# Mixed attention, linear attention and 32 experts on one core: the expert loop written out

## The chip, the cores and the metric

The kernel runs on one core of one Trainium2 chip. The metric is the device time of one execution, in microseconds (us), lower is better. The three timed executions of the kernel before took 1819.9, 1821.0 and 1821.1 us.

## What is computed

One layer over 512 tokens of width 1024, in float32: a mixer (chunked gated linear attention and three groups of dilated attention, gated and merged), then a mixture of experts, each behind a norm and with a residual. The change touches the experts alone:

```python
logits = (xn @ router_w + router_b).astype(jnp.float32)
top_v, top_e = lax.top_k(logits, TOP_K)          # 4 of 32 experts for each token
gates = jax.nn.softmax(top_v, axis=-1)
...
h = xb @ w_gate_up[e] + b_gate_up[e]             # 1024 -> 2048
gate = jnp.minimum(h[:, ::2], SWIGLU_LIMIT)
up = jnp.clip(h[:, 1::2], -SWIGLU_LIMIT, SWIGLU_LIMIT)
act = (up + 1.0) * (gate * jax.nn.sigmoid(SWIGLU_ALPHA * gate))
return act @ w_down[e] + b_down[e]               # 1024 -> 1024
```

Each token's four results are added with their gates as factors. Every expert has 8 MB of gate and up weights and 4 MB of down weights; the kernel reads all 32 experts' weights once, 384 MB.

## The kernel before, in words

The first 690 us or so are the mixer, the router and the lists of each expert's tokens. The expert stage is in `experts` (from L1820). An expert's tokens fill up to 96 slots; more are dealt with in `further_blocks`, behind a test, and that part is not touched.

Weights stream in 1 MB chunks through a ring of 16 buffers (`expert_ring`). An expert has twelve chunks, eight of gate and up and four of down. `chunk_loaded[r]` counts landings in slot r, and the semaphore `used` counts chunks that TensorE has read.

The stage runs in bodies, one for each of experts 0 to 30; expert 31 has an ending of its own. A body e is skewed: it multiplies gate and up of expert e + 1 (its chunks 0 to 7, `gate_up_chunk`, product line L1915) and then down of expert e (its chunks 8 to 11, `down_chunk`, L1924). Between them TensorE turns expert e's activations (`turn_act`, L1888) behind chunks 2 and 3, and expert e + 2's rows (`turn_rows`, L1878) behind chunk 9, where it also starts the next bias products (L1908). Each engine has a body of its own:

- TensorE (`body_pe`): the products above. Before a chunk it waits for its landing (`chunk_here`, L1745 and L1746), before the first for the copied rows (`x_out`), before the ninth for the activations (`aT_out`) and for the copied results of the body before (`y_out`).
- ScalarE (`body_act`): copies turned activations, the sigmoid, copies turned rows, and at the end scales the results out of PSUM (`rows_out`, L1981).
- VectorE (`body_dve`): the indices of expert e + 2 (`list_take`, `pieces_take`), then clamp and product of expert e + 1 (`swiglu`, L2001 and on).
- GpSimd: the gather of expert e + 2's rows (L1796), then the three scatters that add expert e's results in DRAM (L1870).
- SyncE: waits for `used`, then issues the chunk that goes 16 chunks further on (L1743); behind a body's ninth chunk, three small bias loads (L1737).

The order on each engine is written out by hand, and nothing but semaphores ties the engines together. The loop is made in `over_bodies`, for each engine on its own: bodies 0 and 1 are written out (`PEELED`), then a loop of 7 turns holds four bodies (`UNROLL`), then body 30 is written out. L2065 is the loop's `Fori`; its register set-up, addition and branch all stand under that line. In the loop every wait has a value worked out from the turn's number in a register; in bodies written out it is a constant.

```python
def over_bodies(engine, body):
    for e0 in range(PEELED):
        body(engine, e0, 0)
    with engine.Fori(0, TURNS) as i:
        for u in range(self.UNROLL):
            body(engine, PEELED + u, i)
    for e0 in range(PEELED + self.UNROLL * TURNS, LAST):
        body(engine, e0, 0)
```

Of the kernel before, what the change touches and what calls it, by code (L numbers as in the profile page):

```python
# [9 lines left out]
F32R = mybir.dt.float32r  # L10
I32 = mybir.dt.int32
# [5 lines left out]
P = 128  # L17
# [29 lines left out]
N_EXPERTS, TOP_K, FF = 32, 4, D_MODEL  # L47
# [79 lines left out]
class Kernel:  # L127
# [23 lines left out]
    def build(self):  # L151
        nc = self.nc
        with ExitStack() as top:
# [33 lines left out]
            with ExitStack() as late:  # L187
# [7 lines left out]
                with ExitStack() as moe:  # L195
# [11 lines left out]
                    first = [self.sb(moe, f"expert_chunk{j}", [P, 2, self.WIDE]) for j in range(self.GU)]  # L207
# [13 lines left out]
                    self.bias_place = self.sb(moe, "bias_place_r", [P, P], F32R)  # L221
                    self.index = [self.sb(moe, f"row_index{u}", [P, 1], I32) for u in range(self.UNROLL)]
                    self.piece_row = [self.sb(moe, f"piece_row{u}", [P, self.GROUPS], I32) for u in range(self.UNROLL)]
                    self.piece_weight = [self.sb(moe, f"piece_weight{u}", [P, self.GROUPS]) for u in range(self.UNROLL)]
                    self.moe = {n: self.sem("moe_" + n) for n in (
# [1489 lines left out]
    RING = 16  # L1715
    GU, PER_BODY, UNROLL = 8, 12, 4
    PER_TURN = PER_BODY * UNROLL
    PARTS, GROUPS = P // QUARTER, FIRST_SLOTS // QUARTER
# [25 lines left out]

    def chunk_here(self, pe, c, i=0):  # L1745
        pe.wait_ge(self.chunk_loaded[c % self.RING], 16 * (self.PER_TURN // self.RING) * i + 16 * (c // self.RING + 1))  # L1746
        return self.expert_ring[c % self.RING]
# [73 lines left out]
    def experts(self, stack):  # L1821
        nc, t = self.nc, self.t
        E, GU, BODY, TURN, RING = N_EXPERTS, self.GU, self.PER_BODY, self.PER_TURN, self.RING
        G, PARTS, PIECE, Q = self.GROUPS, self.PARTS, self.PIECE, QUARTER
        HELD = G * PIECE
        rows, y, a = (self.h[:, b, :] for b in range(3))
        xT, aT = self.rowsT, self.actT
        as_rows = lambda tile: tile[:].rearrange("p q k n -> p (q k) n")
# [14 lines left out]
        S = self.moe  # L1843
# [4 lines left out]
        part_rows = lambda p: slice(p * Q, (p + 1) * Q)  # L1848
# [55 lines left out]

        def gate_up_bias(pe, e0, i=0):
            pe.wait_ge(self.bias_in[e0 % 2], 16 * G * (self.UNROLL // 2) * i + 16 * G * (e0 // 2 + 1))
            for j, bank in enumerate(h_banks):
                pe.matmul(bank, self.bias_place[part_rows(j), :], self.bias_rows[e0 % 2][part_rows(j), :].bitcast(F32R),  # L1908
                          start=True, stop=False)

        def gate_up_chunk(pe, c, i, k, x=xT):
            w = chunk_here(pe, c, i)
            for j, bank in enumerate(h_banks):
                for p in range(PARTS):
                    last = pe.matmul(bank[part_rows(p), :], x[:, k, part_rows(j)], w[:, p // 2, p % 2 * COLS:(p % 2 + 1) * COLS],  # L1915
                                     start=False, stop=(k == KT - 1))
            last.then_inc(S["used"], 1)

        def down_chunk(pe, c, i, q):
            w = chunk_here(pe, c, i)  # L1920
            for kk in range(2):
                for j in range(G):
                    for p in range(PARTS):
                        last = pe.matmul(y_of(j)[part_rows(p), :], aT[:, q, kk, part_rows(j)], w[:, kk, p * PIECE:(p + 1) * PIECE],  # L1924
                                         start=(q == 0 and kk == 0), stop=(q == 3 and kk == 1))
            last.then_inc(S["used"], 1)
# [8 lines left out]

        def body_pe(pe, e0, i):
            e, more = i * self.UNROLL + e0, e0 < E - 2
            for q in range(BODY):
                c = self.body_chunk(e0, q)
                if q == 0:  # L1940
                    pe.wait_ge(S["x_out"], 2 * e + 4)
                    if e0 == 0:
                        pe.wait_ge(S["gu"], 2)
                        gate_up_bias(pe, 1)
                if q < GU:
                    gate_up_chunk(pe, c, i, q)
                else:
                    if q == GU:
                        pe.wait_ge(S["aT_out"], G * e + G)
                        if e0:  # L1950
                            pe.wait_ge(S["y_out"], G * e)
                    if q == BODY - 2 and e0 == E - 2:
                        turn_act(pe, E - 1, range(2))
                    if q == BODY - 1 and e0 == E - 2:
                        turn_act(pe, E - 1, range(2, G))
                    down_chunk(pe, c, i, q - GU)
                if q == 2:
                    turn_act(pe, e, range(2))
                if q == 3:
                    turn_act(pe, e, range(2, G))  # L1960
                if q == 9 and more:
                    turn_rows(pe, e + 2)
                    pe.wait_ge(S["gu"], 2 * e + 4)
                    gate_up_bias(pe, e0 + 2, i)

# [7 lines left out]

        def rows_out(act, e0, i):
            e = i * self.UNROLL + e0
            act.wait_ge(S["used"], TURN * i + self.body_chunk(e0, BODY - 1) + 1)
            act.wait_ge(S["pieces"], 2 * e + 2)
            if e0:
                act.wait_ge(S["scattered"], 16 * G * e)
            for j in range(G):  # L1980
                act.activation(y[:, j * PIECE:(j + 1) * PIECE], y_of(j), ACT.Copy,  # L1981
                               scale=self.piece_weight[e0 % self.UNROLL][:, j:j + 1]).then_inc(S["y_out"], 1)

        def body_act(act, e0, i):
            e = i * self.UNROLL + e0
            act_back(act, e, aT)
            gate_sigmoid(act, e + 1)
            if e0 < E - 2:
                rows_back(act, e + 2, xT)
            else:  # L1990
                act_back(act, E - 1, as_act(xT))
            rows_out(act, e0, i)

        def swiglu(dve, e, c, i, first=False):
            dve.wait_ge(S["used"], TURN * i + c + 1)
            if not first:
# [13 lines left out]

        def body_dve(dve, e0, i):
            e, more = i * self.UNROLL + e0, e0 < E - 2
            if more:
                u = (e0 + 2) % self.UNROLL
                if e0 > 1:
                    dve.wait_ge(S["scattered"], 16 * G * (e - 1))
                list_take(dve, e + 2, u)
                pieces_take(dve, e + 2, u)  # L2020
            else:
                list_hot(dve, E - 1)
            swiglu(dve, e + 1, self.body_chunk(e0, GU - 1), i)

# [33 lines left out]

        PEELED, LAST = 2, E - 1
        TURNS = (LAST - PEELED) // self.UNROLL  # L2060

        def over_bodies(engine, body):
            for e0 in range(PEELED):
                body(engine, e0, 0)
            with engine.Fori(0, TURNS) as i:  # L2065
                for u in range(self.UNROLL):
                    body(engine, PEELED + u, i)
            for e0 in range(PEELED + self.UNROLL * TURNS, LAST):
                body(engine, e0, 0)

        with nc.Block() as block:
            @block.sync
            def _(sp):
# [8 lines left out]

                def body(sp, e0, i):
                    e = i * self.UNROLL + e0
                    for q in range(BODY):
                        c = self.body_chunk(e0, q)
                        if c < RING:
                            continue
                        sp.wait_ge(S["used"], TURN * i + c - RING + 1)
                        if q < GU:  # L2090
                            self.load_gate_up(sp, c, e + 1, q)
                        else:
                            self.load_down(sp, c, e, q - GU)
                        if q == GU and e0 < E - 2:
                            self.load_bias_rows(sp, e + 2, e0)
                over_bodies(sp, body)
# [19 lines left out]
            def _(pool):  # L2116
# [20 lines left out]

                def body(pool, e0, i):
                    e = i * self.UNROLL + e0
                    if e0 < E - 2:  # L2140
                        gather(pool, e + 2, (e0 + 2) % self.UNROLL)
                    scatter(pool, e, e0 % self.UNROLL)
                over_bodies(pool, body)
# [29 lines left out]
            def _(dve):  # L2173
# [4 lines left out]
                dve.wait_ge(self.normed_stored, 16 * NB)  # L2178
                swiglu(dve, 0, GU - 1, 0, first=True)
                dve.wait_ge(S["lists_in"], 16 * (1 + PARTS))  # L2180
# [36 lines left out]
            def _(pe):  # L2217
# [9 lines left out]
                for c in range(GU):  # L2227
                    gate_up_chunk(pe, c, 0, c, as_rows(aT))
                    if c == 5:
# [288 lines left out]
```

## Time and profile before

| what | value |
|---|---|
| median of three executions | 1821.0 us |
| the profiled execution | 1832.8 us |
| its span, first to last instruction | 1831.0 us |
| mean granted TensorE clock | 0.985 |
| instructions executed | 38017 |
| weight traffic, hardware queue | 479.12 MB |

Rows of the profile are of one execution, which has its own time; a sum made from them is made against 1832.8 us. PE is a matmul of TensorE and PEld a weight load; PEldq, SPq, ACTq, DVEq and POOLq are the sequencers of the engines: waits, register work, branches and the issue of DMAs, which count as no busy time. "Issue" as the end of an idle time means that the engine waited for nothing that the profile shows. In the digits over 40 slices a slice is 45.8 us long. A float32 matmul of the program appears as two in the counts.

### The profile page before, as it was taken

How to read it: one execution, taken by the hardware profiler on the slowest of the kernel's cores; microseconds unless marked ns; L12 is line 12 of the kernel's file. 1: busy time of each engine (PE TensorE's matmuls, PEld its weight loads, DVE VectorE, ACT ScalarE, POOL GpSimd, SP SyncE). 2: the span in 40 equal slices, each digit the busy share in tenths (PEclk: the TensorE clock that was granted, in tenths of full speed). 3: DMA queues.
4: the chain of work that ended last, by engine and by line, in shares of the span. 5: the costliest groups of instructions: out<-in, count | busy, mean ns of one | idle time of the engine just before them, and what ended most of it. 6: DMA issues, size and time to landing. Idle time of an engine off the chain costs nothing.

```text
span 1831.0 us, 38017 instructions
## 1 busy us (share of the span) xinstructions
PE 1767.4 (97%) x16447; PEld 996.1 (54%) x16448; DVE 449.8 (25%) x692; ACT 378.9 (21%) x673; POOL 218.1 (12%) x182
## 2 busy tenths in 40 slices
PE   9999999999999989999999989989999989989997
PEld 7877788898888863433433433434334334334433
DVE  4256255446324540100100100100010001001003
ACT  4254232246422321110101111111111101101111
POOL 1000000000000013121112112112111211211111
PEclk9999999999999989999999999999999999999999
DMA  5321344412223787999989999999999999999973
GB/s 186 123 92 47 120 139 116 122 40 100 92 92 138 270 329 288 384 388 398 394 321 395 394 338 386 397 334 375 397 347 389 389 343 381 392 344 382 397 276 100
DMA packets 112158, 500.47 MB, mean 273 GB/s; under 512 B 19512, under 2 KB 29712, under 8 KB 62400
## 3 DMA queue, kind: packets, MB, share of 16 engines
q1 hardware_dynamic: 92272, 479.12, 68.4%
q0 software_dynamic: 18672, 16.74, 4.5%
q10 hardware_dynamic: 1056, 2.16, 0.5%
q8 instruction: 140, 2.29, 0.5%
q14 instruction: 18, 0.15, 0.0%
HBM read 486.07 MB, written 21.15 MB: 277 GB/s over the span
## 4 chain that ended last, share of the span: by engine, by line
PE 61%; issue 2%; DVE 0%; POOL 0%; ACT 0%; DVEq 0%
PE psum L1915 38%; PE psum L1924 18%; PE psum L1888 2%; PE psum L1878 1%; PE psum L1908 1%; PE psum L1932 1%; PE psum L244 0%; DVE expert_chunk L2056 0%; DVE h_sb L2212 0%; POOL total_rstd L2147 0%; PE psum L2045 0%; PE psum L2039 0%; ACT up_values L2168 0%; DVE gate_values L2212 0%; PE psum L2237 0%
## 5 line engine op out<-in xcount | busy, mean ns | idle before, releaser
L1915 PE MATMUL psum<-expert_chunk,rowsT 128*32 128x512 f32 x2976 | 341.9, 611 | 30.7 <-issue 30.7
L1915 PE MATMUL psum<-expert_chunk_late,rowsT 128*32 128x512 f32 x2976 | 328.5, 593 | 0.0
L2001 DVE TENSOR_SCALAR gate_values<-psum 128x768 f32<-128x768 f32 x32 | 30.6, 958 | 974.9 <-PE psum L1915 974.9
L1870 POOL DMA_INDIRECT residual_rows<-h_sb,piece_row x93 | 145.4, 1564 | 903.9 <-ACT h_sb L1981 830.0
L1915 PEld LDWEIGHTS psum<-expert_chunk,rowsT 128*32 128x32 f32 x2976 | 97.1, 112 | 243.9 <-issue 242.2
L1915 PEld LDWEIGHTS psum<-expert_chunk_late,rowsT 128*32 128x32 f32 x2976 | 93.4, 110 | 202.9 <-issue 200.5
L290 DVE TENSOR_TENSOR chunk_lo<-chunk,chunk_hi 128x2048 fp32r<-128x2048 f32 x48 | 110.0, 2291 | 257.5 <-ACT chunk_hi L286 238.7
L1924 PE MATMUL psum<-expert_chunk_late,activationsT 128*32 128x256 f32 x3072 | 172.2, 380 | 0.0
L1924 PE MATMUL psum<-expert_chunk,activationsT 128*32 128x256 f32 x2880 | 161.3, 380 | 0.0
L321 PE MATMUL psum<-xT_hi,chunk_hi 128*128 128x512 f32 x384 | 150.3, 392 | 4.5 <-DVE chunk_lo L290 2.0
L321 PE MATMUL psum<-xT_hi,chunk_lo 128*128 128x512 f32 x384 | 149.5, 389 | 0.0
L321 PE MATMUL psum<-xT_lo,chunk_hi 128*128 128x512 f32 x384 | 149.5, 389 | 0.0
L1924 PEld LDWEIGHTS psum<-expert_chunk_late,activationsT 128*32 128x32 f32 x3072 | 98.1, 110 | 73.8 <-issue 13.6
L286 ACT CAST chunk_hi<-chunk 128x2048 fp32r<-128x2048 f32 x48 | 91.8, 1913 | 189.5 <-PE psum L321 158.0
L1924 PEld LDWEIGHTS psum<-expert_chunk,activationsT 128*32 128x32 f32 x2880 | 92.1, 110 | 69.3 <-issue 12.6
L321 PE MATMUL psum<-chunk_hi,xT_hi 128*128 128x512 f32 x288 | 113.5, 394 | 2.6 <-ACT gla_v L723 1.5
L321 PE MATMUL psum<-chunk_hi,xT_lo 128*128 128x512 f32 x288 | 112.7, 391 | 0.0
L321 PE MATMUL psum<-chunk_lo,xT_hi 128*128 128x512 f32 x288 | 112.6, 391 | 0.0
L1900 ACT COPY activationsT<-psum 128x256 f32<-128x256 f32 x93 | 31.6, 374 | 338.6 <-PE psum L1888 305.0
L1972 ACT ACTIVATE gate_sigmoid<-gate_values 128x768 f32<-128x768 f32 x32 | 27.1, 847 | 350.0 <-DVE gate_values L2001 350.0
L321 PEld LDWEIGHTS psum<-xT_hi,chunk_hi 128*128 128x128 f32 x384 | 72.1, 188 | 21.3 <-DVE chunk_lo L290 2.7
L321 PEld LDWEIGHTS psum<-xT_hi,chunk_lo 128*128 128x128 f32 x384 | 72.1, 188 | 15.2
(281 smaller groups left out, 1533.1 us busy)
## 6 DMA issues: line engine op xcount, KB each, us to landing
expert_chunk<-in_expert_w_gate_up SPq DMA_DIRECT2D x132, 1024.0 KB
expert_chunk_late<-in_expert_w_gate_up SPq DMA_DIRECT2D x124, 1024.0 KB, 8.3
expert_chunk_late<-in_expert_w_down SPq DMA_DIRECT2D x68, 1024.0 KB, 8.1
expert_chunk<-in_expert_w_down SPq DMA_DIRECT2D x60, 1024.0 KB
chunk<-in_w_in SPq DMA_DIRECT2D x38, 1024.0 KB, 5.1
chunk<-in_w_branch_gla SPq DMA_DIRECT2D x4, 1024.0 KB, 5.1
chunk<-in_w_mix_out SPq DMA_DIRECT2D x4, 1024.0 KB, 5.1
gla_v<-in_x SPq DMA_DIRECT2D x4, 512.0 KB
```

The costliest lines, as they stand in the source:

```text
L286: act.copy(self.whi[c][:], self.raw[c][:]).then_inc(self.hi_done[c], 1)
L290: dve.tensor_tensor(self.wlo[c][:], self.raw[c][:], self.whi[c][:].bitcast(F32), ALU.subtract).then_inc(self.lo_done[c], 1)
L321: last = pe.matmul(bank, stationary, moving, start=(k == 0 and n == 0), stop=(k == KT - 1 and n == 2))
L1870: pool.indirect_dma_start(pieces, bass.IndirectOffsetOnAxis(ap=self.piece_row[u][:, j:j + 1], axis=0), y[:, j * PIECE:(j + 1) * PIECE], No ...
L1878: last = pe.transpose(turned(f)[:, k, :], rows[taken, (HALF_KT * f + k) * P:(HALF_KT * f + k + 1) * P], self.ident[taken, taken])
L1888: last = pe.transpose(turned_act(j)[:, k * P:(k + 1) * P], a[:, (2 * j + k) * P:(2 * j + k + 1) * P], self.ident[:])
L1900: act.copy(dst[:, :, :, part_rows(j)].rearrange("p q k r -> p k q r"), turned_act(j).rearrange("p (k q r) -> p k q r", k=2, q=PARTS)).then ...
L1908: pe.matmul(bank, self.bias_place[part_rows(j), :], self.bias_rows[e0 % 2][part_rows(j), :].bitcast(F32R), start=True, stop=False)
L1915: last = pe.matmul(bank[part_rows(p), :], x[:, k, part_rows(j)], w[:, p // 2, p % 2 * COLS:(p % 2 + 1) * COLS], start=False, stop=(k == KT ...
L1924: last = pe.matmul(y_of(j)[part_rows(p), :], aT[:, q, kk, part_rows(j)], w[:, kk, p * PIECE:(p + 1) * PIECE], start=(q == 0 and kk == 0), ...
L1972: act.activation(sg[:, 0:HELD], gv[:, 0:HELD], ACT.Sigmoid, scale=SWIGLU_ALPHA).then_inc(S["sig"], 1)
L2001: dve.tensor_scalar(by_row(gv), gates_ups[:, :, :, :, 0], SWIGLU_LIMIT, None, ALU.min).then_inc(S["gu"], 1)
```

## The change

All 31 bodies are written out on every engine. `over_bodies` becomes one plain loop of the program that writes the kernel; no `Fori` is left, no branch and no register in the stage's waits, which are on constants throughout. The turn's number `i` goes from all helpers, and `e0`, the body's number within its turn, becomes `e`. `UNROLL`, which was both the bodies per turn and the number of index buffers, is now `BUFFERS` with the same value of 4, so buffers are used as before. Order and number of products, transfers and waits of each body are the same.

```diff
-    GU, PER_BODY, UNROLL = 8, 12, 4
-    PER_TURN = PER_BODY * UNROLL
+    GU, PER_BODY, BUFFERS = 8, 12, 4
...
-    def chunk_here(self, pe, c, i=0):
-        pe.wait_ge(self.chunk_loaded[c % self.RING], 16 * (self.PER_TURN // self.RING) * i + 16 * (c // self.RING + 1))
+    def chunk_here(self, pe, c):
+        pe.wait_ge(self.chunk_loaded[c % self.RING], 16 * (c // self.RING + 1))
         return self.expert_ring[c % self.RING]
...
-        def body_pe(pe, e0, i):
-            e, more = i * self.UNROLL + e0, e0 < E - 2
+        def body_pe(pe, e):
+            more = e < E - 2
...
-        PEELED, LAST = 2, E - 1
-        TURNS = (LAST - PEELED) // self.UNROLL
+        LAST = E - 1

         def over_bodies(engine, body):
-            for e0 in range(PEELED):
-                body(engine, e0, 0)
-            with engine.Fori(0, TURNS) as i:
-                for u in range(self.UNROLL):
-                    body(engine, PEELED + u, i)
-            for e0 in range(PEELED + self.UNROLL * TURNS, LAST):
-                body(engine, e0, 0)
+            for e in range(LAST):
+                body(engine, e)
...
-                def body(sp, e0, i):
-                    e = i * self.UNROLL + e0
+                def body(sp, e):
                     for q in range(BODY):
-                        c = self.body_chunk(e0, q)
+                        c = self.body_chunk(e, q)
                         if c < RING:
                             continue
-                        sp.wait_ge(S["used"], TURN * i + c - RING + 1)
+                        sp.wait_ge(S["used"], c - RING + 1)
...
-                def body(pool, e0, i):
-                    e = i * self.UNROLL + e0
-                    if e0 < E - 2:
-                        gather(pool, e + 2, (e0 + 2) % self.UNROLL)
-                    scatter(pool, e, e0 % self.UNROLL)
+                def body(pool, e):
+                    if e < E - 2:
+                        gather(pool, e + 2, (e + 2) % self.BUFFERS)
+                    scatter(pool, e, e % self.BUFFERS)
```

The other helpers (`gate_up_bias`, `gate_up_chunk`, `down_chunk`, `rows_out`, `body_act`, `swiglu`, `body_dve`) lose `i` in the same way.

## Rows read from the trace of the kernel before

**Rows 1.** The page's head: span, then busy tenths in 40 slices.

```profile
span 1831.0 us, 38017 instructions
PE   9999999999999989999999989989999989989997
PEclk9999999999999989999999999999999999999999
DMA  5321344412223787999989999999999999999973
```

**Rows 2.** The page's chain that ended last: share of the span by engine, by line.

```profile
PE 61%; issue 2%; DVE 0%; POOL 0%; ACT 0%; DVEq 0%
PE psum L1915 38%; PE psum L1924 18%; PE psum L1888 2%; PE psum L1878 1%; PE psum L1908 1%; PE psum L1932 1%; PE psum L244 0%; DVE expert_chunk L2056 0%; DVE h_sb L2212 0%; POOL total_rstd L2147 0%; PE psum L2045 0%; PE psum L2039 0%; ACT up_values L2168 0%; DVE gate_values L2212 0%; PE psum L2237 0%
```

**Rows 3.** Windows, cut at starts of chunk 4; busy us and counts; columns in first line.

```profile
core 0: us, PE busy (x) PEld busy (x) DVE busy (x) ACT busy (x) POOL busy (x), PEclk, DMA share, GB/s
724.73:892.60 167.87, 167.87 (x2009) 68.38 (x2013) 19.75 (x35) 19.65 (x45) 28.89 (x20) 1.00 1.01 388
892.60:934.14 41.54, 36.48 (x405) 14.09 (x409) 3.95 (x7) 3.93 (x9) 5.75 (x4) 0.92 0.91 340
1034.85:1075.39 40.54, 35.89 (x405) 13.93 (x409) 3.95 (x7) 3.93 (x9) 5.75 (x4) 0.96 0.93 352
1176.09:1218.27 42.18, 35.85 (x406) 15.14 (x409) 3.95 (x7) 3.92 (x9) 5.77 (x4) 0.92 0.91 342
1318.98:1358.72 39.74, 35.27 (x406) 14.32 (x409) 3.95 (x7) 3.93 (x9) 5.75 (x4) 0.96 0.95 354
1459.42:1500.90 41.48, 36.32 (x405) 13.94 (x409) 3.95 (x7) 3.92 (x9) 5.75 (x4) 0.92 0.93 347
1601.62:1642.64 41.02, 35.98 (x405) 14.21 (x409) 3.95 (x7) 3.93 (x9) 5.75 (x4) 0.96 0.93 338
1642.64:1776.92 134.28, 134.28 (x1608) 54.70 (x1612) 16.18 (x26) 15.71 (x36) 21.94 (x15) 1.00 0.98 375
```

**Rows 4.** The merged chain at the first turn edge: start us, us, what.

```profile
909.46 5.32 PE psum L1924 x96
914.77 5.06 issue
919.84 10.63 PE psum L1915 x72
```

**Rows 5.** The loop's branch by engine: count, duration ns min/median/max, first and last start.

```profile
L2065 SPq COMPARE_BRANCH  x7: 40/45/50, 870.1 to 1720.9; - x7
L2065 PEldq COMPARE_BRANCH  x7: 83/5932/7367, 913.4 to 1764.2; - x7
L2065 ACTq COMPARE_BRANCH  x7: 40/45/50, 915.1 to 1765.8; - x7
```

**Rows 6.** The page's DMA queues: packets, MB, share of 16 engines.

```profile
q1 hardware_dynamic: 92272, 479.12, 68.4%
q8 instruction: 140, 2.29, 0.5%
```

**Rows 7.** ScalarE's waits from 859 to 892.6 us: us in total, times, longest.

```profile
ACT h_sb L1981 <- PE psum L1924: 5.3, 1, 5.3
ACT rowsT L1895 <- PE psum L1878: 3.8, 1, 3.8
```

**Rows 8.** Window behind the first edge's gap, columns as in rows 3.

```profile
919.84:930.47 10.63, 10.63 (x73) 2.82 (x74) 0.00 (x0) 0.00 (x0) 3.28 (x3) 0.74 0.64 172
```

**Rows 9.** SyncE's queue: waits (us, times, longest), and landings of L1743.

```profile
SPq L1743 <- PE psum L1915: 538.2, 241, 10.6
SPq L1743 <- PE psum L1924: 282.2, 120, 3.6
DMA to landing us min/median/max: 6.1/8.2/12.5
```

**Rows 10.** Windows of the first three bodies behind an edge, columns as in rows 3.

```profile
934.14:967.71 33.57, 33.57 (x405) 13.68 (x409) 3.95 (x7) 3.93 (x9) 5.75 (x4) 1.00 0.98 366
967.71:1001.27 33.56, 33.56 (x405) 13.67 (x409) 3.95 (x7) 3.93 (x9) 5.75 (x4) 1.00 1.01 396
1001.27:1034.85 33.58, 33.58 (x406) 13.68 (x409) 3.95 (x7) 3.93 (x9) 5.75 (x4) 1.00 1.02 388
```

More of the change, by code:

```diff
@@ L221, in build @@
                     self.bias_place = self.sb(moe, "bias_place_r", [P, P], F32R)
-                    self.index = [self.sb(moe, f"row_index{u}", [P, 1], I32) for u in range(self.UNROLL)]
-                    self.piece_row = [self.sb(moe, f"piece_row{u}", [P, self.GROUPS], I32) for u in range(self.UNROLL)]
-                    self.piece_weight = [self.sb(moe, f"piece_weight{u}", [P, self.GROUPS]) for u in range(self.UNROLL)]
+                    self.index = [self.sb(moe, f"row_index{u}", [P, 1], I32) for u in range(self.BUFFERS)]
+                    self.piece_row = [self.sb(moe, f"piece_row{u}", [P, self.GROUPS], I32) for u in range(self.BUFFERS)]
+                    self.piece_weight = [self.sb(moe, f"piece_weight{u}", [P, self.GROUPS]) for u in range(self.BUFFERS)]
                     self.moe = {n: self.sem("moe_" + n) for n in (
@@ L1822, in experts @@
         nc, t = self.nc, self.t
-        E, GU, BODY, TURN, RING = N_EXPERTS, self.GU, self.PER_BODY, self.PER_TURN, self.RING
+        E, GU, BODY, RING = N_EXPERTS, self.GU, self.PER_BODY, self.RING
         G, PARTS, PIECE, Q = self.GROUPS, self.PARTS, self.PIECE, QUARTER
@@ L1901, in act_back, with gate_up_bias, gate_up_chunk @@
                          turned_act(j).rearrange("p (k q r) -> p k q r", k=2, q=PARTS)).then_inc(S["aT_out"], 1)
-        def gate_up_bias(pe, e0, i=0):
-            pe.wait_ge(self.bias_in[e0 % 2], 16 * G * (self.UNROLL // 2) * i + 16 * G * (e0 // 2 + 1))
+        def gate_up_bias(pe, e):
+            pe.wait_ge(self.bias_in[e % 2], 16 * G * (e // 2 + 1))
             for j, bank in enumerate(h_banks):
-                pe.matmul(bank, self.bias_place[part_rows(j), :], self.bias_rows[e0 % 2][part_rows(j), :].bitcast(F32R),
+                pe.matmul(bank, self.bias_place[part_rows(j), :], self.bias_rows[e % 2][part_rows(j), :].bitcast(F32R),
                           start=True, stop=False)
-        def gate_up_chunk(pe, c, i, k, x=xT):
-            w = chunk_here(pe, c, i)
+        def gate_up_chunk(pe, c, k, x=xT):
+            w = chunk_here(pe, c)
             for j, bank in enumerate(h_banks):
@@ L1917, in gate_up_chunk, with down_chunk @@
             last.then_inc(S["used"], 1)
-        def down_chunk(pe, c, i, q):
-            w = chunk_here(pe, c, i)
+        def down_chunk(pe, c, q):
+            w = chunk_here(pe, c)
             for kk in range(2):
@@ L1934, in last_down_chunk @@
             last.then_inc(S["used"], 1)
-        def body_pe(pe, e0, i):
-            e, more = i * self.UNROLL + e0, e0 < E - 2
+        def body_pe(pe, e):
+            more = e < E - 2
             for q in range(BODY):
-                c = self.body_chunk(e0, q)
+                c = self.body_chunk(e, q)
                 if q == 0:
                     pe.wait_ge(S["x_out"], 2 * e + 4)
-                    if e0 == 0:
+                    if e == 0:
                         pe.wait_ge(S["gu"], 2)
@@ L1945, in body_pe @@
                 if q < GU:
-                    gate_up_chunk(pe, c, i, q)
+                    gate_up_chunk(pe, c, q)
                 else:
@@ L1949, in body_pe @@
                         pe.wait_ge(S["aT_out"], G * e + G)
-                        if e0:
+                        if e:
                             pe.wait_ge(S["y_out"], G * e)
-                    if q == BODY - 2 and e0 == E - 2:
+                    if q == BODY - 2 and e == E - 2:
                         turn_act(pe, E - 1, range(2))
-                    if q == BODY - 1 and e0 == E - 2:
+                    if q == BODY - 1 and e == E - 2:
                         turn_act(pe, E - 1, range(2, G))
-                    down_chunk(pe, c, i, q - GU)
+                    down_chunk(pe, c, q - GU)
                 if q == 2:
@@ L1963, in body_pe @@
                     pe.wait_ge(S["gu"], 2 * e + 4)
-                    gate_up_bias(pe, e0 + 2, i)
+                    gate_up_bias(pe, e + 2)
         def gate_sigmoid(act, e, first=False):
@@ L1972, in gate_sigmoid, with rows_out @@
             act.activation(sg[:, 0:HELD], gv[:, 0:HELD], ACT.Sigmoid, scale=SWIGLU_ALPHA).then_inc(S["sig"], 1)
-        def rows_out(act, e0, i):
-            e = i * self.UNROLL + e0
-            act.wait_ge(S["used"], TURN * i + self.body_chunk(e0, BODY - 1) + 1)
+        def rows_out(act, e):
+            act.wait_ge(S["used"], self.body_chunk(e, BODY - 1) + 1)
             act.wait_ge(S["pieces"], 2 * e + 2)
-            if e0:
+            if e:
                 act.wait_ge(S["scattered"], 16 * G * e)
@@ L1981, in rows_out, with body_act @@
                 act.activation(y[:, j * PIECE:(j + 1) * PIECE], y_of(j), ACT.Copy,
-                               scale=self.piece_weight[e0 % self.UNROLL][:, j:j + 1]).then_inc(S["y_out"], 1)
-        def body_act(act, e0, i):
-            e = i * self.UNROLL + e0
+                               scale=self.piece_weight[e % self.BUFFERS][:, j:j + 1]).then_inc(S["y_out"], 1)
+        def body_act(act, e):
             act_back(act, e, aT)
             gate_sigmoid(act, e + 1)
-            if e0 < E - 2:
+            if e < E - 2:
                 rows_back(act, e + 2, xT)
@@ L1991, in body_act, with swiglu @@
                 act_back(act, E - 1, as_act(xT))
-            rows_out(act, e0, i)
-        def swiglu(dve, e, c, i, first=False):
-            dve.wait_ge(S["used"], TURN * i + c + 1)
+            rows_out(act, e)
+        def swiglu(dve, e, c, first=False):
+            dve.wait_ge(S["used"], c + 1)
             if not first:
@@ L2011, in swiglu, with body_dve @@
             dve.tensor_tensor(a[:, 0:HELD], uv[:, 0:HELD], sg[:, 0:HELD], ALU.mult).then_inc(S["act"], 1)
-        def body_dve(dve, e0, i):
-            e, more = i * self.UNROLL + e0, e0 < E - 2
+        def body_dve(dve, e):
+            more = e < E - 2
             if more:
-                u = (e0 + 2) % self.UNROLL
-                if e0 > 1:
+                u = (e + 2) % self.BUFFERS
+                if e > 1:
                     dve.wait_ge(S["scattered"], 16 * G * (e - 1))
@@ L2022, in body_dve @@
                 list_hot(dve, E - 1)
-            swiglu(dve, e + 1, self.body_chunk(e0, GU - 1), i)
+            swiglu(dve, e + 1, self.body_chunk(e, GU - 1))
         def further_experts(dve):
@@ L2081, in _ @@
                              ).then_inc(S["tables_in"], 16)
-                def body(sp, e0, i):
-                    e = i * self.UNROLL + e0
+                def body(sp, e):
                     for q in range(BODY):
-                        c = self.body_chunk(e0, q)
+                        c = self.body_chunk(e, q)
                         if c < RING:
                             continue
-                        sp.wait_ge(S["used"], TURN * i + c - RING + 1)
+                        sp.wait_ge(S["used"], c - RING + 1)
                         if q < GU:
@@ L2093, in body @@
                             self.load_down(sp, c, e, q - GU)
-                        if q == GU and e0 < E - 2:
-                            self.load_bias_rows(sp, e + 2, e0)
+                        if q == GU and e < E - 2:
+                            self.load_bias_rows(sp, e + 2, e)
                 over_bodies(sp, body)
@@ L2136, in _ @@
                                    ).then_inc(S["lists_in"], 16)
-                def body(pool, e0, i):
-                    e = i * self.UNROLL + e0
-                    if e0 < E - 2:
-                        gather(pool, e + 2, (e0 + 2) % self.UNROLL)
-                    scatter(pool, e, e0 % self.UNROLL)
+                def body(pool, e):
+                    if e < E - 2:
+                        gather(pool, e + 2, (e + 2) % self.BUFFERS)
+                    scatter(pool, e, e % self.BUFFERS)
                 over_bodies(pool, body)
@@ L2178, in _ @@
                 dve.wait_ge(self.normed_stored, 16 * NB)
-                swiglu(dve, 0, GU - 1, 0, first=True)
+                swiglu(dve, 0, GU - 1, first=True)
                 dve.wait_ge(S["lists_in"], 16 * (1 + PARTS))
@@ L2227, in _ @@
                 for c in range(GU):
-                    gate_up_chunk(pe, c, 0, c, as_rows(aT))
+                    gate_up_chunk(pe, c, c, as_rows(aT))
                     if c == 5:
```

## The prediction

> **What bounds the kernel now.** I read the head of the page first, then the chain of work that ended last, then windows over the expert stage, then one turn edge in the merged chain, and last the rows of the loop's own instructions and of the DMA queues.
>
> The head shows PE busy in nearly every slice, with a granted clock of nine tenths or more and DMA engines almost as full from slice 20 on [rows 1]. So two resources are candidates for the bound of the expert stage: TensorE, and the DMA engines that bring 12 MB of weights per expert. The chain decides between them: 61% of the span is PE, nearly all of it the two product lines of the experts, L1915 (gate and up) and L1924 (down), and 2% is "issue", time in which PE waited for nothing that the profile shows. No DMA has a share worth a row [rows 2]. This 2% is the part to look for.
>
> A body is easiest to cut at the start of chunks 4 to 7 (96 matmuls in a row in the merged chain). The first five intervals between such starts take 167.87 us together, 33.57 us each, and PE is busy in all of it; the last four take 134.28 us, again 33.57 each, again all busy [rows 3]. Six intervals are longer: 41.54, 40.54, 42.18, 39.74, 41.48 and 41.02 us [rows 3]. There are 31 bodies: 2 peeled, 7 turns of 4, 1 more. Seven turns have six taken branches back, and the long intervals are four bodies apart from 892.60 on, which is where the first turn ends. In the first five intervals PE passes from peeled bodies, which wait on constants as all bodies will after the change, into the loop, whose waits have register values. The length is the same. So register waits and register arithmetic cost PE nothing today, and the whole stake of the change is the six edges.
>
> At the first edge the last down products end, then follow 5.06 us of "issue", then the first 72 matmuls of the next body take 10.63 us [rows 4]. An undisturbed body has no such gap. On PE's sequencer the branch of L2065 lasted 5.9 us in the median and 7.4 at most; the shortest, 83 ns, is the seventh, which is not taken. The same branch on ACT took 40 to 50 ns [rows 5]. Only PE stalls. A body is 405 matmuls and 409 weight loads on PE [rows 3], a turn over 3200 instructions. The instruction queue moved 140 packets, 2.29 MB [rows 6]; the program executed 38017 instructions [rows 1], some 270 per packet. That is about one fetch of each executed instruction, so PE's loop code is brought in again on each turn, and PE's branch waits for that. This cause is my reading; the cost stands without it.
>
> **The change part by part, against the profiled execution** (1832.8 us, span 1831.0, 1.8 us around it; the median of the unprofiled runs is 1821.0, 11.8 lower).
>
> Removed: six taken branches on PE. The six long intervals sum to 246.50 us; six plain ones are 201.44 (6 x 33.574, from 167.87/5). The excess is 45.1 us [rows 3]. It has two terms. Idle: 246.50 less PE busy (36.48 + 35.89 + 35.85 + 35.27 + 36.32 + 35.98 = 215.79) is 30.7 us. Slow clock: 215.79 - 201.44 = 14.4 us, in which PE was busy but late. The granted clock of these intervals is 0.92 to 0.96, against 1.00 in all others [rows 3]: after each gap there is a stretch at 1.2 GHz in place of 2.4. With no gap before it, I expect the clock to stay at 2.4 GHz, as it does over five bodies and over four without a gap, so this term goes too. Sum: -30.7 - 14.4 = -45.1 us.
>
> One rule of the Trainium skill speaks against this sum. The rows show taken branches of 5.6 to 7.4 us on PE. The page Advanced Engine Details and Errata, section Control Flow Timing, gives a compare-and-branch about 108 ns. By it six branches would be worth 0.6 us and the change could not be measured; by the rows it is 45 us. The ACT rows fit the page, the PE rows do not, and PE is the engine of the chain.
>
> Removed: the register moves, additions and comparisons on all engines. On PE they are worth nothing, as the equal intervals show. On ACT, DVE, POOL and SP they lie in waits: ACT waits 5.3 us for the last down products and 3.8 us for the turned rows in each body [rows 7]. Cost 0; bound from below, a few tenths of a us in the last rows of a body, from above 0.
>
> Added: code. All engines now run through new instructions for 31 bodies. PE did so before too, since its code was fetched on every turn: about 814/270, or 3 packets per body, before and after. Between edges these fetches cost nothing visible: PE is busy for 33.57 of 33.57 us while they run. ACT, DVE, POOL and SP, of which the loop's code seems to have stayed in place (branches of 40 to 80 ns), now fetch afresh. Beside its 9 busy instructions per body ACT has about as many waits; that is 2 to 3 packets over the stage. DVE (7 busy ones) and POOL (4) have no more, SP perhaps six. No row shows the price of such a straight-line crossing on these engines in this stage. From below it is 0 (PE crosses without loss); from above, the whole branch stall of 6 us less the wait that covers it (5.3 us on ACT), some 1 us for each of ACT's three, plus the same on DVE: 5 us. I take 0, by the row that is nearest in kind (straight-line crossing under the same traffic), and keep 5 for the range. SP has other cover: it issues 16 chunks ahead.
>
> Changed: the pace of the transfers. Now the DMA engines get 8 us of rest at each edge: in the 10.6 us behind the first gap they moved only 172 GB/s, at a share of 0.64 [rows 8]. That rest goes. SP waited 361 times (241 + 120) for PE to free a slot, of 384 chunks, so the queue runs on demand, and a chunk lands 8.2 us after its issue (12.5 at most) [rows 9]. A slot is issued 16 chunks before its use, 16/12 x 33.57 = 44.8 us, so weights lie ready 36 us before PE wants them, 32 at worst. If the DMA engines were a little too slow without the rest, this lead would pay first: 31 bodies could each be 1.1 us short before PE waited once. Over five bodies without rest they moved 388 GB/s at full PE pace. Cost 0.
>
> Moved: nothing; the order on each queue (the three bias loads behind a body's ninth chunk, the gather before the scatter on POOL) is the same. Buffers of the index and piece lists are picked by the same remainder of the expert.
>
> What is late next when the edges are gone: PE itself, at 33.57 us per body. Forecast for the profiled execution: 1832.8 - 45.1 = 1787.7 us (span 1785.9); for the median: 1821.0 - 45.1 = **1776 us**. The last step assumes that the profiler's 11.8 us lie elsewhere. If all of it sat in the edges, the unprofiled gain would be 33.3 us and the median 1788.
>
> **The rivals.**
> A. Forecast, edges gone and nothing given back: 1776 us, with the bounds above 1770 to 1790.
>
> B. The change does not do what it says: the fetch stall stays with straight code. The stall is not the branch but the traffic: a packet of instructions queues behind weight packets on DMA engines at 0.98 to 1.02 share [rows 10]. Place: each of PE's some 93 packets. A stall of 0.45 us on each would eat the 45 us: 1821. Against it: within five bodies some 15 such packets passed and PE was never idle. For it: only that fetch and weights share the engines.
>
> C. The DMA engines become the bound. A turn (934.14 to 1075.39) moves 366 x 33.57 + 396 x 33.56 + 388 x 33.58 + 352 x 40.54 = 52.9 MB, 13.2 per body, at 374 GB/s on average [rows 3, 10]. If 374 were what they can keep up, a body would need 35.35 us; 31 x 1.78 = 55 us short, of which the lead of 36 pays, leaving 19 us of waits: 1776 + 19 = 1795.
>
> D. The same mechanism further on, and slower than before: the sustained rate drops when the rest at the edges is gone. It decides from 31 x (13.2/rate - 33.57) = 45 + 36, a body of 36.2 us or 365 GB/s. At 352 (the rate of an interval with an edge) a body is 37.6 us, 124 us short, less 36 of lead: +88 on 1776, that is 1864. Place: PE's wait for its chunk at L1915, from about body 10 on. For it: shares of 1.01 and 1.02 [rows 10] leave no visible room. Against it: 388 to 396 GB/s in windows without an edge, landings that stay at some 8 us, and a share that follows demand (0.64 where PE is slow).
>
> **How the numbers follow.** A 0.86, B 0.04 (1821, and milder forms around 1800 to 1820), C 0.04, D 0.02; 0.04 stays for a larger gain than the sum, down to 1765, should unprofiled edges cost more than profiled ones. The range of 8 in 10 is that of A with its bounds, 1769 to 1791. The measurement can tell about 0.2%, 3.6 us, from no change. Faster by more than that: A, C, the larger gain and half of B, 0.96; same, the other half of B, 0.02; slower, D, 0.02.
>
> **What would show it.** Right: no L2065 rows; all intervals between starts of chunks 4 to 7 are 33.57 us with PE busy all through; the granted clock is 1.00 from 730 to 1750 us; "issue" falls from 2% of the chain to about 0.2%; chunks land 8 us after issue up to the last body; the stage before 700 us is unchanged. Wrong: idle time of PE before L1915 or L1924 with "issue" as the releaser at intervals of some 270 instructions (B); intervals that lengthen from the tenth body on, with waits on expert_chunk and landings of 20 to 40 us (C, D); a body of 33.57 us everywhere and yet a smaller gain in the median, which would put the profiler's cost into the edges.

## Result and profile after

The changed kernel is faster: the ratio of its executions to those of the kernel before is 0.9776, 95% interval 0.9757 to 0.9795. The medians are 1779.3 us against 1820.5 us, 41 us apart; both leave out one execution of 5021 us, of which no trace exists and which none of the ten later executions of this kernel repeated. The forecast was 1776, its range 1769 to 1791. The profiled execution took 1779.3 us, with a span of 1777.5 us; for it the forecast was 1787.7.

The head of the page, for comparison with [rows 1]: PE at nine in every slice but the last, a granted clock of nine tenths or more in all but the last, and the DMA engines at nine tenths from slice 17 to slice 38. Under it the chain by engine, against [rows 2]: the 2% of "issue" has become 0%.

```profile
span 1777.5 us, 36227 instructions
...
PE   9999999999999999999999999999999999999997
...
PEclk9999999999999999999999999999999999999998
DMA  5321254411334398999999999999999999999963
...
PE 61%; DMA 1%; DVE 0%; POOL 0%; issue 0%; ACT 0%; DVEq 0%; POOLq 0%
```

Windows of the kernel after, again cut at starts of chunk 4, with the columns of [rows 3]: the first five intervals, the other 25, and all that follows.

```profile
715.49:883.33 167.84, 167.84 (x2009) 68.39 (x2013) 19.72 (x35) 19.64 (x45) 29.90 (x21) 1.00 1.01 388
883.33:1722.49 839.16, 839.16 (x10029) 341.91 (x10033) 99.02 (x173) 98.23 (x225) 142.89 (x99) 1.00 1.01 391
1722.49:1777.50 55.01, 42.08 (x355) 19.57 (x354) 15.76 (x20) 9.28 (x18) 8.80 (x7) 0.90 0.26 83
```

839.16/25 is 33.57 us, with PE busy in all of it and the clock at 1.00. Not one of the 30 intervals is longer. From the first start to the last the profile before needed 1776.92 - 724.73 = 1052.19 us, the profile after 1722.49 - 715.49 = 1007.00 us: 45.2 us less.

The two spans differ by more, 53.5 us, and the medians by less. The profile before starts its bodies 9.2 us later (724.73 against 715.49), and that is no work of the change. In the merged chain of the kernel before, ahead of the first body, PE issues a few matmuls at a time with gaps of "issue" between them (start us, us, what):

```profile
694.84 0.38 issue
695.22 1.08 PE psum L1915 x5
696.29 0.37 issue
696.66 1.06 PE psum L1915 x4
697.72 0.35 issue
698.08 0.49 PE psum L1878 x4
698.57 1.63 issue
```

This creep is discussed below: it came on some chips and not on others, in both kernels. Behind the last start the kernel after is 0.9 us slower (55.01 us; 1831.0 - 1776.92 = 54.1 before).

### The profile page after: what moved, and what is told of

Its sections match the earlier page's. It is cut to its first block, busy times and chain, and to the rows that moved or that the text cites. A ratio compares the mean times of both kernels' runs of the same rounds, so it can differ in the third digit from the quotient of the medians.

```text
span 1777.5 us, 36227 instructions
## 1 busy us (share of the span) xinstructions
PE 1747.7 (98%) x16447; PEld 991.4 (56%) x16448; DVE 449.8 (25%) x692; ACT 379.0 (21%) x673; POOL 218.8 (12%) x182
## 4 chain that ended last, share of the span: by engine, by line
PE 61%; DMA 1%; DVE 0%; POOL 0%; issue 0%; ACT 0%; DVEq 0%; POOLq 0%
PE psum L1914 37%; PE psum L1923 18%; PE psum L1887 2%; PE psum L1877 1%; PE psum L1907 1%; PE psum L1931 1%; DMA h_sb<-normed_rows,row_index 1%; PE psum L244 0%; DVE expert_chunk L2053 0%; DVE h_sb L2201 0%; POOL total_rstd L2136 0%; PE psum L2042 0%; PE psum L2036 0%; ACT up_values L2157 0%; DVE gate_values L2201 0%
## 5 line engine op out<-in xcount | busy, mean ns | idle before, releaser
L1914 PE MATMUL psum<-expert_chunk,rowsT 128*32 128x512 f32 x2976 | 328.6, 593 | 0.0
L1914 PEld LDWEIGHTS psum<-expert_chunk,rowsT 128*32 128x32 f32 x2976 | 93.5, 110 | 202.4 <-issue 199.7
```

## Experiments

The runs were made in three groups, each on a chip of its own, and each is compared with the kernel before on that chip. It took 1831.2 us there in the first group (the second trace, the first repeat of the changed kernel, one turn, and PE alone), 1821.5 in the second (the second repeat, PE alone again, its converse, and the kernel with little traffic) and 1831.2, one execution, in the third (the other four, one execution each).

**The same kernel before, a second trace.**

> The kernel before once more, for a second trace. In the first trace PE crept for some 9 us between 694 and 702 us, ahead of the loop, issuing single matmuls with 0.4 to 1.6 us of issue between them. Theory: that was an accident of that one execution, so it is gone here (profiled time 1819 to 1826 us) while six long intervals of 39 to 43 us stay. Rival: it is the profiler's own and comes back (1830 us or more).

It took 1832.0 us: on this chip the creep was there again, in the kernel before and in the kernel after. The chain of the second trace, before the first body:

```profile
700.52 0.47 issue
700.99 0.37 PE psum L1878 x2
701.36 0.55 PE psum L1915
701.91 1.21 issue
703.11 1.77 PE psum L1915 x4
```

The nine executions of the kernel before beside it took 1828 to 1835 us, so the 10 us are no accident of one execution, and since most of these were not profiled, not the profiler's either. My theory missed, and so did the rival, whose 1830 us or more came true for another reason: here nearly every execution seems to have had the creep. The edges were of use: the six long intervals were 40.92, 40.42, 41.28, 40.22, 41.83 and 40.30 us, an excess of 43.5 us, against 45.1 in the first trace.

**The changed kernel, twice more.**

> The changed kernel once more. Theory: all 30 intervals between starts of chunks 4 to 7 are 33.57 us and the ratio to the kernel before is 0.975 to 0.979 (1776 to 1782 us). Rival (the transfers are near their limit, a matter of the chip or the hour): some interval is longer than 34 us, with a wait on a DMA.

Ratio 0.9769 (0.9756 to 0.9783), 1789.8 against 1831.2 us. Here too the creep cost some 10 us ahead of the first body, and all intervals were 33.57 us. The ratio is as expected; the times of 1776 to 1782 us that I expected here, with one turn and with PE alone are not, since the kernel before took 10 us more on this chip too.

> The changed kernel, timed beside the next one on one chip. Ratio to before 0.975 to 0.979, as so far; the intervals of all bodies 33.57 us.

Ratio 0.9763 (0.9745 to 0.9780), 1778.1 against 1821.5 us, no creep, all intervals 33.57 us. The gain is the same with the creep (41.4 us) and without (43.4 us).

**Registers without a taken branch.** 28 bodies in the turn; the buffers stay at four.

```diff
-    GU, PER_BODY, UNROLL = 8, 12, 4
+    GU, PER_BODY, UNROLL, BUFFERS = 8, 12, 28, 4
```

> The kernel before with 28 bodies in the turn: the loop, its registers and its branch stay, but the branch is never taken. Theory (the taken branches carry the whole cost, register waits none): the time of the changed kernel, 1776 to 1782 us, all intervals 33.57. Rival (waits and addresses in registers cost PE or SP something): part of the 41 us stays, 1785 to 1815.

Ratio 0.9757 (0.9742 to 0.9773), beside 0.9769 for the changed kernel on this chip. All intervals are 33.57 us, and the branch of PE, which falls through, is short:

```profile
L2065 PEldq COMPARE_BRANCH  x1: 76/76/76, 1719.7 to 1719.7; - x1
```

So waits and addresses in registers cost nothing that these runs can tell. It is the taken branch.

**Whose branch.** First only PE's bodies are written out, then only the others'.

```diff
         def over_bodies(engine, body):
+            if engine in (nc.tensor,):       # the converse: (nc.sync, nc.scalar, nc.vector, nc.gpsimd)
+                for e0 in range(LAST):
+                    body(engine, e0, 0)
+                return
```

> Only PE's bodies are written out; SP, ACT, DVE and POOL keep the loop of seven turns. Theory (only PE's taken branch stalls): the time of the changed kernel, 1776 to 1782 us. Rival (another engine's turn holds PE up too, SP's above all): intervals of over 33.6 us remain at the turns and the time is 1785 or more.

> Only PE's bodies written out, timed beside the changed kernel. It was 3.8 us faster than the changed kernel where both ran before, of which the two traces show 0.9 us behind the last body. Theory (the rest was spread between executions): 0 to 2 us faster than the changed kernel. Rival (written-out code on the other engines costs time ahead of or behind the bodies): 3 to 5 us faster again.

> The converse: PE keeps the loop of seven turns, SP, ACT, DVE and POOL are written out. Theory (PE's branch is the whole cost): the time of the kernel before within 0.2%, six intervals of 40 to 43 us, PE branches of 5.5 to 7.4 us. Rival (the turn of another engine adds to the edge): 5 us or more faster than before.

PE alone written out gives the whole gain: 0.9748 (0.9733 to 0.9763) beside the changed kernel's 0.9769, and 0.9761 (0.9743 to 0.9778) beside its 0.9763 on the next chip. All intervals are 33.57 us. In both traces it is 0.9 us shorter than the changed kernel behind the last body; more than that the second pair does not show, so I don't call it faster. The converse gives nothing: 0.9996 (0.9984 to 1.0007), with PE's branches as before and six intervals of 39.79 to 41.37 us, an excess of 41.0 us:

```profile
L2069 PEldq COMPARE_BRANCH  x7: 83/5537/6092, 902.5 to 1749.2; - x7
```

**Three turns.** Eight bodies in a turn, two taken branches.

> The kernel before with eight bodies in a turn: three turns, two taken branches, and five bodies written out behind. Theory (a fixed price per taken branch): two intervals of 40 to 43 us, each branch 5.2 to 7.4 us though the turn is twice as long, 28 to 31 us faster than before. Rival (the price grows with the length of the turn's code): branches of 10 us or more.

It took 1805.1 us, 26.2 less than before on this chip. Two intervals are long, 41.56 and 41.38 us, an excess of 15.8 us where six edges had 41.0 to 45.1. The branches were as long as ever, though a turn has twice the code:

```profile
L2065 PEldq COMPARE_BRANCH  x3: 83/5707/6050, 1048.4 to 1601.3; - x3
```

A price per taken branch, then, that does not grow with the code. The gain of 26 lies under my 28 to 31; it is four edges at 6.5 us, near the cheap end of the edges in the traces (6.2 to 8.6 us), though its own two cost 7.9 us each. It is one execution against one, and 0.8 us of it went behind the last body (see below).

**Is the wait one for code that queues behind weights?** Two experiments: take the traffic away, and take the code away. The traffic first; from chunk 16 on a load fills 16 partitions, so most weights are old ones and the results others.

```diff
-        sp.dma_start(self.expert_ring[r][:], src).then_inc(self.chunk_loaded[r], 16)
+        n = P if c < self.RING else 16
+        sp.dma_start(self.expert_ring[r][0:n], src[0:n]).then_inc(self.chunk_loaded[r], 16)
```

> The kernel before with the loop, but from the 17th chunk on each weight load fills 16 of 128 partitions instead of all (an eighth of the traffic; the other rows keep old weights, so the results are others). PE's work and code are the same. Theory (PE's branch waits for its code, and the fetches queue behind weight packets): the branch falls from 5.5-7.4 us to 1-3 us, the intervals at the edges to 34-36 us. Rival (the branch has a price of its own, or the fetch takes that long on idle DMA engines too): it stays at 5 us or more.

Between both. PE's branch, then a turn of this kernel in the windows' columns (62 GB/s in place of some 374), then the idle time at its first edge in the merged chain:

```profile
L2066 PEldq COMPARE_BRANCH  x7: 83/3692/4175, 903.4 to 1736.0; - x7
903.40:1041.91 138.51, 135.07 (x1612) 54.97 (x1605) 15.79 (x28) 15.72 (x36) 23.01 (x16) 1.00 0.26 62
904.75 2.97 issue
```

The six taken branches lasted 3.3 to 4.2 us in the trace instead of 5.2 to 7.4, the long intervals were 37.70 to 38.56 us. So about two thirds of the stall is there with this little traffic, and a third (some 2 us) goes with the traffic, which I had made the main thing. Theory (1 to 3 us) and rival (5 us or more) both missed; the answer lies between them.

Then the code. PE multiplies one of four column parts, except where a sum opens or closes, so the experts' results are partial; in the second kernel one part of one group of three.

```diff
                 for p in range(PARTS):
+                    if x is xT and k < KT - 1 and p > 0:      # down_chunk likewise; the second kernel: (p > 0 or j > 0)
+                        continue
```

> The kernel before with its loop, but of each chunk's four column parts PE multiplies only the first, except in the chunks that open and close a sum (so the experts' results are partial). A turn on PE falls from some 3250 instructions to some 1400; weights stream as before. Theory (each turn's code is fetched again because it is too long for what the sequencer holds, and that holds less than this): PE's branch stays at 5 us or more. Rival (the sequencer holds some 2000 instructions): the branch falls to 0.1 to 0.3 us.

> The same with one column part of one group only: some 970 instructions per turn on PE. Both as for the run before; if the branch is short here and long there, the limit lies between 970 and 1400 instructions, if long in both, below 970.

The theory fell, the rival held. The taken branch is short as soon as the turn is short, under full traffic:

```profile
L2069 PEldq COMPARE_BRANCH  x7: 76/208/220, 908.4 to 1712.7; - x7
L2069 PEldq COMPARE_BRANCH  x7: 76/207/227, 875.4 to 1673.1; - x7
```

(the first row is of the kernel with a quarter, the second of the one with least; the 76 ns are the branch that is not taken). Counted in the trace between two branches PE runs 3240 instructions in the kernel before, 6478 with eight bodies, 1368 and 952 in these two. Up to 1368 the branch takes 0.2 us, from 3240 on 5.2 to 7.4 us. The loop's code fits what PE's sequencer holds, or is brought in again; the limit lies somewhere between 1368 and 3240.

The packets of the instruction queue show this directly. Queue q8 brings PE's code: it moved 125 packets in the changed kernel and with PE alone written out, and 140 in the kernel before [rows 6] and with all but PE written out. So its count goes by PE alone. In order, the pages of the changed kernel and of those with eight bodies, with a quarter and with least work have:

```profile
q8 instruction: 125, 2.05, 0.5%
q8 instruction: 131, 2.15, 0.5%
q8 instruction: 37, 0.61, 0.1%
q8 instruction: 34, 0.56, 0.1%
```

Laid out in time, these packets are 15 in each turn of four full bodies and 28 in each turn of eight that follows a taken branch. With a quarter of the products there is none from the first branch at 908.4 us to the last at 1712.7; with least work there is one, in the first of the six turns. The same packets time the stall. In the four traces with a taken branch behind a long turn under full traffic (20 branches) an instruction packet begins 2.9 to 5.0 us after the branch does, and the branch ends 2.3 to 2.6 us after that packet began. With little traffic the packet begins after 1.0 to 1.5 us, and the branch ends 2.3 to 3.0 us later. So what the traffic adds is the time until the packet begins.

The Trainium skill, page Runtime: NRT & Kernel Launch, section Instruction fetch mechanics, gives PE room for 2048 instructions, which lies between this case's 1368 and 3240. The same section's remark that only two blocks of 256 instructions are held would make a turn of 1368 stall; on PE the 208 ns above speak against it.

With one part in four the body was hardly shorter: 134.05 us per turn, 33.51 per body, PE busy throughout. The chain shows why: the products for which PE needs 72 matmuls and 7.72 us in the full kernel are 18 matmuls there, and they take the same time.

```profile
909.74 7.72 PE psum L1917 x18
```

The four column parts of a product run side by side (in the timeline of the kernel before, four of 0.59 us start together every 0.43 us), so leaving out three of them saves no time. With least work the transfers took over: in the six turns PE waits 254 us for the landing of weights. Windows of the second kernel, a first turn and the next five:

```profile
875.37:1008.48 133.11, 90.56 (x468) 26.00 (x465) 15.79 (x28) 15.89 (x36) 23.01 (x16) 0.78 1.02 409
1008.48:1673.07 664.59, 454.53 (x2308) 130.03 (x2305) 79.35 (x138) 79.74 (x180) 115.06 (x80) 0.78 1.02 399
```

PE is busy for two thirds, the DMA share is 1.02 throughout, and a body takes (133.11 + 664.59)/24 = 33.24 us. That is the floor which the transfers set. PE's 33.57 us lie 1% above it.

**Idle time without a branch.** The changed kernel with a wait that holds PE for the landing of the last scatters:

```diff
                     pe.wait_ge(S["x_out"], 2 * e + 4)
+                    if e in range(6, LAST, 4):
+                        pe.wait_ge(S["scattered"], 16 * G * e)
```

> The changed kernel (no loop) with one more wait on PE, ahead of bodies 6, 10, 14, 18, 22 and 26: until the scatters of the body before have landed. PE then stands still for some 8 to 10 us six times, with no branch. Theory (the slow clock at the edges follows from the idle time alone): each of the six intervals is longer than 33.57 by the idle time and 2 to 4 us of slow clock on top, 1835 to 1855 us in all. Rival (the slow issue behind a branch is the fetch's own): only the idle time is added and the first 72 matmuls behind it take 7.7 us.

It forms a seventh gap, since body 30 is in that range too; all seven intervals are long, and the time is 1866.8 us, outside the 1835 to 1855 that I expected for six. Windows of the gap before body 6 and of the 72 matmuls behind it:

```profile
912.60:921.97 9.37, 0.00 (x1) 0.03 (x1) 0.00 (x0) 1.20 (x3) 5.75 (x4) 0.67 0.75 240
921.97:931.85 9.88, 9.88 (x73) 2.82 (x74) 0.00 (x0) 0.00 (x0) 0.00 (x0) 0.80 0.52 172
```

The 72 matmuls took 9.88 us at a granted clock of 0.80, 7.72 us in a body without a gap. With no branch in the stage, 2.2 us of slow clock follow the idle time; at an edge of the kernel before it was 14.4/6 = 2.4 us on average. The rival expected 7.7 us here and is refuted. The intervals were 43.78 to 45.96 us. Of my sum the number of gaps was off, and their length at the upper end.

## Why the prediction was right, point by point

**The bound.** PE bounds the stage, as read from [rows 2] and [rows 3]: the body stays at 33.57 us in every trace with full work.

**The sum, -45.1 us.** Right between the two profiles: 1052.19 - 1007.00 = 45.2. Both terms went, idle time and slow clock, and the experiment with gaps shows that the second follows from the first. As a forecast of the median it was 2 to 4 us too large: 40.8 us by the ratio of the first comparison, some 42 and 43 on the later chips. The mis-sized term is the price of an edge. I took it from one execution, which held the dearest edges of the three traces with seven full turns on PE under full traffic: 45.1, 43.5 and 41.0 us. Six draws of 6.2 to 8.6 us are a thin basis, and my lower bound of the gain should have come from this spread.

**The 11.8 us between profile and median.** Here the step itself failed, though within the range. I called them the profiler's and considered that they might sit in the edges. The profiled execution of the changed kernel was no slower than the others (1779.3 among 1777.7 to 1781.6), nor were the later ones. The bodies started 9.2 us later in the profile before than in the one after; with the creep as its cause that is most of the 11.8, and rows of the stage before 725 us would have shown it to me. The three executions of 1819.9 to 1821.1 us have no trace, so that they had no creep is inferred from their times. The forecast assumed the 11.8 us outside the edges, which fits. That the creep would be absent from the profile after was not forecast, and so the profiled execution came out 8.4 us below its 1787.7.

**Cause: code fetched again on each turn.** Read from the packet count [rows 6] and the branch rows [rows 5], said to be a reading; the kernels with shorter turns and their packets show it. My count of 270 instructions per packet came out near the truth by luck: it divides the instructions of all engines by q8's packets. PE's own are 33334 to 140 packets before, 238 each, and 33214 to 125 after, 266 each; a taken branch comes with some two and a half packets more than straight code. Not foreseen: that the price is mostly the fetch itself, and only a third of it the traffic. Nor did I look at PE's other loop. The trace of the kernel before has seven taken branches on L363, in the mixer, behind turns of some 196 instructions; they took 0.21 to 0.24 us, which already said that a taken branch of PE is short where the turn is short.

```profile
L363 PEldq COMPARE_BRANCH  x10: 83/215/240, 105.4 to 531.5; - x10
```

ACT's 40 to 50 ns do not fit the 108 ns quoted beside them as well as the prediction says; they are less than half.

**Register work on PE, cost 0.** Right, shown by the kernel with one turn.

**New code on ACT, DVE, POOL and SP, 0 to 5 us.** Zero within the bodies. Behind the last body 0.9 us appeared: from the last start of chunk 4 to the end it is 54.0 to 54.1 us in both traces of the kernel before, in both with PE alone written out and in those with little traffic and with a quarter, and 54.9 to 55.0 us in all three of the changed kernel, in the one-turn kernel, in the one with gaps, in the one with eight bodies and in the one that loops on PE alone. The split goes by the code of the other engines: four bodies in their loop, or more. All of it lies in the landing of the last output, 2.7 us after its issue in the first set and 3.5 to 3.6 us after it in the second; in the second alone packets of the other instruction queue, q14, begin in that time. The amount lies in the bound, at a place that I had not named; that these packets are its cause was not tested.

**Transfers, cost 0; rivals C and D.** Right in the time, with a remainder. Landings of L1743 before were 8.2 us in the median [rows 9] and stayed near 8 us throughout. After, they drift. The answers for issues between 760 and 900 us and between 1600 and 1730 us:

```profile
DMA to landing us min/median/max: 6.4/8.4/9.4
DMA to landing us min/median/max: 8.3/10.5/11.6
```

2.1 us over some 25 bodies: the queue falls behind by under 0.1 us per body and pays from a lead of 36. The mechanism of rival C exists, at a twentieth of the dose that I gave it. The rest at the edges was being used, but it was not needed. It was also less than the 8 us that I gave it: at a share of 0.91 in an interval of 41.54 us [rows 3], the engines were free for some 4 us. Rival D's rate of 352 GB/s never came: the transfers alone sustain 399.

**Rival B** is refuted: 94 instruction packets of q8 pass in the 1007 us between first and last start, and PE has no idle time. (Its price was slightly off: 93 stalls of 0.45 us are 42 us, not 45.)

## What to carry to other kernels

Read the branch's own row before judging a loop: on PE, which bounds this stage, a taken branch took 0.2 us where the turn had up to 1368 instructions and 5.2 to 7.4 us where it had 3240 or more, plus some 2 us of half clock behind the gap. Write out that engine alone, or keep its turn short; on the other engines, which wait anyway, the loops cost nothing here. And before removing one engine's gaps, look for what used them: here the transfers were 1% from being the bound.

## What was not expected of the hardware

Ahead of the expert bodies PE sometimes issues a few matmuls at a time, from about 694 to 704 us, with up to 1.6 us between them. The first start of chunk 4 is at 714 to 715 us in all four traces of the second group, at 723 to 726 us in all four of the first, whatever the kernel, and at 719 to 725 us in all four of the third; of the two first traces the one had the creep (725 us) and the other not (715 us). So it goes with the chip rather than with the kernel. Semaphores that PE waits for do not explain it (the profile ends these gaps with "issue"). What does was not tested and stays open; it is as large as a quarter of the gain of this change.
